# Block 2 of a two-block network: masks behind the level products, inverses turned from the bank, both output gates of seven pairs by quarters

## The chip, the cores and the metric

The kernel runs on one core of a Trainium2 chip. The time is device time in microseconds (us). A core has TensorE (PE in the profile; PEld are its weight loads), VectorE (DVE), ScalarE (ACT), GpSimd (POOL) and SyncE (SP), which issues the loads. They run side by side and wait for one another by semaphores. TensorE writes into eight PSUM banks of 512 f32 per partition, which VectorE and ScalarE read. Everything is f32.

## The reference

The program computes two blocks for 256 tokens of width 1024. The change touches only block 2:

```python
p = jnp.einsum('bsd,de->bse', h, w_in[l])
c_val, c_gate, c_og, ts, r_og, g_conv, g_rwkv = jnp.split(p, SPLITS, axis=-1)
y_conv = _conv_branch(c_val, c_gate, c_og, ...)         # 31 taps, layer norm
y_rwkv = _rwkv7_branch(ts, r_og, ...)                   # the scan below
m = jax.nn.sigmoid(g_conv) * y_conv + jax.nn.sigmoid(g_rwkv) * y_rwkv
x = x + gate[:, None, :] * jnp.einsum('bsd,de->bse', m, w_out[l])

def step(state, inp):                                   # for each token, 16 heads of 64
    r_t, w_t, k_t, v_t, kk_t, b_t = inp
    sk = jnp.einsum('bhvk,bhk->bhv', state, kk_t)
    state = (state * w_t[:, :, None, :] - sk[..., None] * b_t[:, :, None, :]
             + v_t[..., None] * k_t[:, :, None, :])
    return state, jnp.einsum('bhvk,bhk->bhv', state, r_t)
```

## The kernel before, in words

Block 2 goes through eight pairs j = 0 to 7 of heads (128 channels on 128 partitions, 256 tokens along the free side). For each pair nine slices of the input weights, 1024x128 each, are loaded by SyncE into nine slots and multiplied with `hT`, the normed input: VAL and GATE (convolution), R, K, V, OGP and ROG (inner gates), GCP and GRP (the two output gates). `projection` does one of them as 8 matmuls with 256 moving columns and puts the result into bank 0 or 1 by turns (`PLACE`). `read_out` makes it wait until the projection two places earlier has been read out of the bank.

The scan is done in four chunks of 64 tokens. Within a chunk the strictly triangular matrix N of each head is inverted as I + N by doubling, levels 1 to 5. ScalarE copies N from bank 2 to `Nt`. GpSimd makes seven tensors of it (`pool_rwkv`): the first level `Z0` in two operations, and `Nm`, the blocks of N that belong to each level, in five. VectorE transposes `Z0` to `X0` (`turned(0)`). For a level l, TensorE multiplies its blocks with X (`grown(l)`, L1116), VectorE adds the unit matrix (L2449), TensorE multiplies with Z (`inverted(l)`, L1128, at the last level L1130), ScalarE copies what is new of the result from bank 3 to `Xs` (L1633), and VectorE transposes `Xs` to the next Z (`turned(l)`, L2455).

At the same time the pair before, p = j - 1, goes through its four chunks in order (`forced`, `solved`, `outcome` on TensorE; `state` on VectorE, L2442 for the first chunk, multiplies the product S by the decay; `St` is what `forced(c)`, L1064, needs).

`pe_rwkv` is TensorE's queue for a pair, written out by hand: the small products of both pairs in a fixed order, and between them `fill(n)`, which takes n matmuls from the generator `behind`. In pair j this gives the five projections of the next pair (VAL, GATE, K, R, V) and then OGP, ROG, GCP, GRP of its own. The numbers are `FILL = (0, 12, 11, 12, 11, 13, 13)`. Pair 7 has no next pair and fills less. `dve_rwkv` and `act_rwkv` are the queues of VectorE and ScalarE, also written by hand: between the small steps VectorE does the 31 taps of the convolution (`taps`, L2389, 128x256 each with two SBUF inputs), makes the operands of the next pair, and multiplies the inner gates (`og_silu`, `rg_silu`, L2467). ScalarE's queue ends a pair with `half_gate` for GCP and GRP, a tanh out of the bank to `GC` and `GR`. SyncE's queue loads a slot when its projection of the pair before has been done (`load_projection`).

Seven products by quarters are already used in block 1, the feed-forward part and the convolution's output (`quarter_product`, L819; `quarter_sums`, L2121, for the sums of quarters of `hT`).

## Time and profile before

| | us |
|---|---|
| median of 3 runs (1078.93 to 1079.96) | 1079.80 |
| the profiled execution | 1079.88 |
| its span, first to last instruction | 1078.10 |
| TensorE busy | 1065.6 (99%) |
| VectorE busy | 720.0 (67%) |
| ScalarE busy | 235.3 (22%) |
| GpSimd busy | 149.7 (14%) |
| granted TensorE clock, mean | 0.999 |

Block 2 from its first projection to the end of the scan takes about 400 us of the span. A line such as L972 is the line of the kernel before; lines of helpers stand for every caller. In a timeline, start and duration are us from the span's start, x16 is a number of merged instructions, and brackets show how long the engine had been idle and who released it. A recorded matmul's end is modelled, so distances are better read from start to start. Each f32 matmul is two instructions in the trace.

### The profile page before, as it was taken

Reading aid. Unit: us, or ns where it says so; the run is one execution under the profiler, and the core shown is the slowest. Engines: PE = TensorE matmul, PEld = TensorE weight load, DVE = VectorE, ACT = ScalarE, POOL = GpSimd, SP = SyncE. Lnnn points to the kernel's source line nnn. Section 1 sums busy time; section 2 is a strip of 40 time slices with the busy share of each in tenths; the row PEclk is TensorE's granted clock in tenths of the full one; section 3 lists DMA queues with packets and bytes.
Section 4 is the critical chain, followed back from the end, with each engine's and each line's share of the span. In section 5 each row is a group of like instructions: output and inputs, shape, how many; then the busy total and the mean of one; then the engine's idle time right before and its main releaser. Section 6 shows DMA issues by size and latency. Waiting matters only on the chain.

```text
span 1078.1 us, 21003 instructions
## 1 busy us (share of the span) xinstructions
PE 1065.6 (99%) x8606; PEld 910.8 (84%) x8606; DVE 720.0 (67%) x1624; ACT 235.3 (22%) x614; POOL 149.7 (14%) x204
## 2 busy tenths in 40 slices
PE   9999999999999999999999999999999999999997
PEld 7899899998998589999744988888888888887983
DVE  4476674766744377777657768666667667666885
ACT  4131130312210020010101422323232232323101
POOL 1101000000036221100160022020202202020042
PEclk9999999999999999999999999999999999999999
DMA  8676566553347346555446233233332322161251
GB/s 286 236 274 250 188 213 215 161 196 98 138 144 262 124 135 215 193 189 182 168 170 259 79 117 99 89 108 99 99 104 94 111 87 80 27 249 40 79 157 40
DMA packets 62769, 163.20 MB, mean 151 GB/s; under 512 B 8625, under 2 KB 22865, under 8 KB 62674
## 3 DMA queue, kind: packets, MB, share of 16 engines
q1 hardware_dynamic: 61666, 160.22, 44.7%
q8 instruction: 69, 1.13, 0.4%
q10 hardware_dynamic: 1008, 1.63, 0.4%
q14 instruction: 26, 0.21, 0.1%
HBM read 160.73 MB, written 1.11 MB: 150 GB/s over the span
## 4 chain that ended last, share of the span: by engine, by line
PE 91%; DVE 6%; DMA 2%; issue 1%; ACT 0%; DVEq 0%; ACTq 0%
PE bank L819 22%; PE bank L972 20%; PE bank L471 16%; PE bank L885 6%; DVE arena L2389 3%; PE bank L631 3%; PE bank L751 2%; PE bank L794 2%; PE bank L1128 2%; PE bank L1285 2%; PE bank L1116 2%; PE bank L1007 1%; PE bank L947 1%; DMA slots<-in_w_br 1%; PE bank L547 1%; PE bank L953 1%
## 5 line engine op out<-in xcount | busy, mean ns | idle before, releaser
L972 PE MATMUL bank<-hT,slots 128*128 128x256 f32 x1120 | 254.6, 382 | 0.0
L972 PEld LDWEIGHTS bank<-hT,slots 128*128 128x128 f32 x1120 | 209.8, 190 | 28.8
L471 PE MATMUL bank<-hT,slots 128*128 128x256 f32 x544 | 119.7, 379 | 0.0
L471 PEld LDWEIGHTS bank<-hT,slots 128*128 128x128 f32 x544 | 103.0, 190 | 14.4 <-issue 0.6
L2389 DVE SCALAR_TENSOR_TENSOR arena<-padA,par,arena 128x256 f32<-128x256 f32 x232 | 113.9, 552 | 0.0
L819 PE MATMUL bank<-arena,slots 128*128 128x128 f32 x768 | 95.6, 275 | 0.0
L819 PE MATMUL bank<-hT,slots 128*128 128x128 f32 x736 | 91.8, 276 | 0.2 <-DVE arena L1937 0.2
L819 PEld LDWEIGHTS bank<-arena,slots 128*128 128x128 f32 x768 | 90.9, 192 | 0.5
L819 PEld LDWEIGHTS bank<-hT,slots 128*128 128x128 f32 x736 | 86.7, 192 | 1.1 <-issue 1.1
L471 PE MATMUL bank<-arena,slots 128*128 128x256 f32 x304 | 66.5, 380 | 0.5 <-DMA slots<-in_w_br 0.5
L471 PEld LDWEIGHTS bank<-arena,slots 128*128 128x128 f32 x304 | 57.5, 190 | 9.0 <-DMA slots<-in_w_br 1.3
L885 PE MATMUL bank<-slots,arena 128*128 128x512 f32 x128 | 55.4, 592 | 0.0
L2894 POOL TENSOR_TENSOR arena<-arena 128x256 f32<-128x256 f32 x8 | 5.8, 729 | 343.4 <-ACT arena L1650 343.4
L885 PEld LDWEIGHTS bank<-slots,arena 128*128 128x128 f32 x128 | 24.2, 190 | 30.1 <-issue 25.6
L2455 DVE STREAM_TRANSPOSE arena<-arena 128x256 f32<-128x256 f32 x40 | 17.7, 442 | 35.8 <-ACT arena L1633 35.0
L1858 DVE TENSOR_SCALAR arena<-bank 64x256 f32<-64x256 f32 x24 | 10.1, 422 | 38.3 <-PE bank L471 37.9
L2892 POOL TENSOR_TENSOR arena<-arena 128x256 f32<-128x256 f32 x40 | 34.3, 888 | 0.0
L819 PE MATMUL bank<-x,slots 128*128 128x128 f32 x256 | 33.9, 275 | 0.1
L819 PE MATMUL bank<-x,arena 128*128 128x128 f32 x256 | 33.8, 275 | 0.0
L819 PEld LDWEIGHTS bank<-x,slots 128*128 128x128 f32 x256 | 31.2, 192 | 0.3 <-DVE arena L1948 0.3
L819 PEld LDWEIGHTS bank<-x,arena 128*128 128x128 f32 x256 | 31.2, 192 | 0.0
L1902 DVE SCALAR_TENSOR_TENSOR adaA<-arena,sc,adaA 128x1024 f32<-128x1024 f32 x24 | 30.7, 1279 | 0.1
(449 smaller groups left out, 1741.3 us busy)
## 6 DMA issues: line engine op xcount, KB each, us to landing
slots<-in_w_rwkv SPq DMA_DIRECT2D x72, 512.0 KB, 3.6
slots<-in_w_heads SPq DMA_DIRECT2D x68, 512.0 KB, 4.5
slots<-in_w_gu SPq DMA_DIRECT2D x44, 512.0 KB, 4.5
arena<-in_ada_w SPq DMA_DIRECT2D x24, 512.0 KB, 5.4
slots<-in_w_down SPq DMA_DIRECT2D x20, 512.0 KB, 4.3
slots<-in_w_br SPq DMA_DIRECT2D x32, 256.0 KB, 2.8
slots<-in_w_out SPq DMA_DIRECT2D x16, 512.0 KB, 4.1
slots<-in_w_y SPq DMA_DIRECT2D x16, 512.0 KB, 5.2
```

Of the source, the lines that this page charges most:

```text
L471: end = e.matmul(psum, w[:, k * P:(k + 1) * P], rhs[:, k, :], start=k == 0, stop=k == kt - 1)
L631: end = e.matmul(view3(bank[5][:, t * T:(t + 1) * T], P), hT[:, k, t * P:(t + 1) * P], slots[:, BV:CV + 1, k * P:(k + 1) * P], start=k == ...
L751: return e.matmul(bank[DOWN_BANK[m]][:, :], *sides, start=j == 0, stop=j == OUT_PAIRS - 1)
L794: end = e.matmul(psum[:, tokens(t)], w[:, k * P:(k + 1) * P], hT[:, k, tokens(t)], start=k == 0, stop=k == KT - 1)
L819: end = e.matmul(out, w[:, k * P:(k + 1) * P], rhs[:, k, :], start=k == 0, stop=k == 3)
L885: return e.matmul(bank[DOWN_BANK[m]][:, :], *sides, start=j == 0, stop=j == DOWN - 1)
L972: end = e.matmul(proj(w, q), slot[w][:, k * P:(k + 1) * P], hT[:, k, :], start=k == 0, stop=k == KT - 1)
L1116: end = e.matmul(bank[2][r, c * CHUNK:(c + 1) * CHUNK], Nm[r, (l - 1) * CHUNKS + c, :], Xs[r, c, :], start=True, stop=True)
L1128: end = e.matmul(chunks(half(3))[r, c, :], Z[r, c, :], Gs[r, c, :], start=True, stop=True)
L1902: e.scalar_tensor_tensor(out=third, in0=adaW[n % 2], scalar=sc[:, 2 * i + n // 3:2 * i + n // 3 + 1], in1=third, op0=ALU.mult, op1=ALU.add ...
L2389: e.scalar_tensor_tensor(out=o, in0=src, scalar=w, in1=o, op0=ALU.mult, op1=ALU.add).then_inc(*dve.step(f"tap{n}.{q}"))
L2892: e.tensor_tensor(Nm[:, (l - 1) * CHUNKS:l * CHUNKS, :], Nt, each(cst2_of("off", CHUNK, l * CHUNK)), ALU.mult).then_inc(*pool.step(f"Nm{l} ...
```

## The change

Four things, all in block 2.

1. *Gates by quarters, pairs 0 to 6.* GCP and GRP of a pair are no longer two projections but one `own_gate_pair`: the two weight slices and `hT` are each taken as 2x2 quarters, and seven products of 4 matmuls with 128 columns (Winograd's form) take the place of eight. Three go to the first bank, four to the second. VectorE makes four sums of weight quarters per pair (`slice_sum`, 128x512; 0 behind `turned(1)`, 1 and 2 behind `turned(2)`, 3 behind `turned(4)`) and, once, four sums of quarters of `hT` (`bt`) at the end of `dve_first`. ScalarE copies the first product (`bp1`), VectorE adds (`first_quarter` at the end of the pair, `other_quarters` behind `forced(0)` of the next), and ScalarE does both tanh in the next pair, from SBUF, behind its two copies of bank 2. `read_out` waits for these sums. The generator yields every two matmuls: 14 steps for 16.
2. *Masks behind the products.* GpSimd masks N to its strict triangle, adds the unit and makes Z0 of it: three operations. `grown(l)` multiplies with all of I + N, and VectorE's operation behind it multiplies by a mask (`within`) where it added the unit.
3. *Inverses turned from the bank.* `turned(l)` transposes bank 3 and waits for TensorE; ScalarE's copy to `Xs` waits for the transpose.
4. *Loads.* The slot of GCP is reloaded after the end of both gates; the first loads of the output part wait for the last own gates.

```diff
-    put("off_first", (i == t + 1) & (i % 2 == 1))
-    for l in range(LEVELS):
+    put("first", (i == t) | (i == t - 1) & (t % 2 == 1))
+    for l in range(1, LEVELS):
         n = 1 << l
-        c[:, CCOL["off"] + l * CHUNK:CCOL["off"] + (l + 1) * CHUNK] = \
-            (i // (2 * n) == t // (2 * n)) & (i // n % 2 == 0) & (t // n % 2 == 1)
+        at = CCOL["within"] + (l - 1) * CHUNK
+        c[:, at:at + CHUNK] = (i == t) | (i // (2 * n) == t // (2 * n)) & (t // n % 2 == 0) & (i // n % 2 == 1)
...
-        Nm = carve((LEVELS - 1) * CHUNKS, CHUNK)
...
+        bt = [slot[9 + n // 2][:, n % 2 * 512:(n % 2 + 1) * 512].rearrange("p (k n) -> p k n", n=P) for n in range(4)]
+        bs = [slot[11][:, 0:512], slot[11][:, 512:], adaA[:, 2 * D:2 * D + 512]]
+        def own_gates(j, n):
+            at, far = 3 * KT * T + j * T + n * P, KT * T + (P if n == 0 else -P)
+            return arena[:, at:at + 2 * far].rearrange("p (a b) -> p a b", a=2)[:, :, 0:P]
...
+                if w in (GCP, GRP) and q < LAST:
+                    e.wait_ge(*dve.upto(f"bq11.{q}" if w == GCP else f"bq1221.{q}"))
+                elif w in (OGP, ROG, LNSUM, LNVAR):
...
+        def gate_banks_of(q):
+            return [view3(bank[PLACE[w, q] % 2][:, :], P) for w in (GCP, GRP)]
+        def own_gate_pair(e, q):
+            one, two = gate_banks_of(q)
+            low, high = hT[:, 0:4, :], hT[:, 4:8, :]
+            first, second = (slot[w] for w in (GCP, GRP))
+            parts = ((one, 0, first[:, 0:512], low[:, :, tokens(0)]), (one, 1, first[:, 512:], high[:, :, tokens(0)]), (one, 2, bs[0], bt[1]),
+                     (two, 0, second[:, 0:512], bt[0]), (two, 1, bs[1], bt[2]), (two, 2, bs[2], high[:, :, tokens(1)]), (two, 3, second[:, 512:], bt[3]))
+            for n, (out, at, w, rhs) in enumerate(parts):
+                if n == 0:
+                    e.wait_ge(*in_slot[GCP].upto(f"rw{GCP}.{q}"))
+                    read_out(e, PLACE[GCP, q] - 2)
+                if n == 2:
+                    e.wait_ge(*dve.upto("bt4"))
+                    e.wait_ge(*dve.upto(f"bs4.{q}"))
+                if n == 3:
+                    read_out(e, PLACE[GRP, q] - 2)
+                for k in range(4):
+                    end = e.matmul(out[:, at, :], w[:, k * P:(k + 1) * P], rhs[:, k, :], start=k == 0, stop=k == 3)
+                    if k == 3 and n in (2, 6):
+                        end.then_inc(*pe.step(f"b126.{q}" if n == 2 else f"p{GRP}.{q}"))
+                    if k % 2:
+                        yield
...
-                for w in OWN:
+                for w in (OGP, ROG):
                     yield from projection(e, w, j)
+                yield from own_gate_pair(e, j)
...
-                    e.wait_ge(*pool.upto(f"Nm1.{j}"))
+                    e.wait_ge(*pool.upto(f"Nd.{j}"))
...
-                        end = e.matmul(bank[2][r, c * CHUNK:(c + 1) * CHUNK], Nm[r, (l - 1) * CHUNKS + c, :], Xs[r, c, :], start=True, stop=True)
+                        end = e.matmul(bank[2][r, c * CHUNK:(c + 1) * CHUNK], Nt[r, c, :], Xs[r, c, :], start=True, stop=True)
...
-                e.wait_ge(*pe.upto(f"XZ{l}.{j}"))
+                e.wait_ge(*dve.upto(f"Z{l}.{j}"))
...
+            if levels and chain:
+                for w, to in (("gc", GC[:, p, :]), ("gr", GR[:, p, :])):
+                    e.wait_ge(*dve.upto(f"bq1221.{p}"))
+                    e.activation(to, to, ACT.Tanh, scale=0.5).then_inc(*act.step(f"{w}.{p}"))
...
+                    e.wait_ge(*pe.upto(f"b126.{j}"))
+                    e.activation(GC[:, j, P:], gate_banks_of(j)[0][:, 0, :], ACT.Copy).then_inc(*act.step(f"bp1.{j}"))
...
+            quarter_sums(e, bt, "bt", (act.upto("norm4.s3.1"), dve.upto("norm4.s7.1"), pe.upto("lora")))
...
-                e.tensor_tensor(Gs, chunks(half(2)), each(cst2_of("unit")), ALU.add).then_inc(*dve.step(f"G{l}.{j}"))
+                e.tensor_tensor(Gs, chunks(half(2)), each(cst2_of("within", CHUNK, (l - 1) * CHUNK)), ALU.mult).then_inc(*dve.step(f"G{l}.{j}"))
...
+                if l:
+                    e.wait_ge(*pe.upto(f"XZ{l}.{j}"))
+                    e.transpose(flat(Zs[j % 2]), half(3)).then_inc(*dve.step(f"Z{l}.{j}"))
+                else:
+                    e.wait_ge(*pool.upto(f"Z0.{j}"))
+                    e.transpose(flat(Xs), flat(Zs[j % 2])).then_inc(*dve.step(f"X0.{j}"))
...
+                if k == 0:
+                    e.wait_ge(*in_slot[GCP].upto(f"rw{GCP}.{j}"))
+                    e.wait_ge(*in_slot[GRP].upto(f"rw{GRP}.{j}"))
+                    e.tensor_tensor(bs[1], a11, a21, ALU.subtract).then_inc(*dve.step(f"bs3.{j}"))
+                elif k == 1:
+                    e.wait_ge(*dve.upto(f"bs3.{j}"))
+                    e.tensor_tensor(a21, a21, a22, ALU.add).then_inc(*dve.step(f"bs1.{j}"))
+                elif k == 2:
+                    e.wait_ge(*dve.upto(f"bs1.{j}"))
+                    e.tensor_tensor(bs[0], a21, a11, ALU.subtract).then_inc(*dve.step(f"bs2.{j}"))
+                else:
+                    e.wait_ge(*dve.upto(f"bs2.{j}"))
+                    e.tensor_tensor(bs[2], a12, bs[0], ALU.subtract).then_inc(*dve.step(f"bs4.{j}"))
...
+            def first_quarter(q):
+                e.wait_ge(*act.upto(f"bp1.{q}"))
+                e.tensor_tensor(own_gates(q, 0), GC[:, q, P:].unsqueeze(1).to_broadcast([P, 2, P]), gate_banks_of(q)[0][:, 1:3, :],
+                                ALU.add).then_inc(*dve.step(f"bq11.{q}"))
...
+            def other_quarters(q):
+                two = gate_banks_of(q)[1]
+                e.wait_ge(*pe.upto(f"p{GRP}.{q}"))
+                e.wait_ge(*dve.upto(f"bq11.{q}"))
+                e.tensor_tensor(own_gates(q, 1), GR[:, q, P:].unsqueeze(1).to_broadcast([P, 2, P]), two[:, 0:2, :],
+                                ALU.add).then_inc(*dve.step(f"bu43.{q}"))
+                e.wait_ge(*dve.upto(f"bu43.{q}"))
+                e.tensor_tensor(GR[:, q, P:], GR[:, q, 0:P], two[:, 0, :], ALU.add).then_inc(*dve.step(f"bq22.{q}"))
+                e.wait_ge(*dve.upto(f"bq22.{q}"))
+                e.tensor_tensor(own_gates(q, 1), own_gates(q, 1), two[:, 2:4, :], ALU.add).then_inc(*dve.step(f"bq1221.{q}"))
...
+                other_quarters(p)
+                slice_sum(0)
+                slice_sum(2)
+                slice_sum(3)
+                first_quarter(j)
...
-            e.tensor_tensor(Zs[j % 2], Nt, each(cst2_of("off")), ALU.mult).then_inc(*pool.step(f"Z0.m.{j}"))
-            e.wait_ge(*pool.upto(f"Z0.m.{j}"))
-            e.tensor_tensor(Zs[j % 2], Zs[j % 2], each(cst2_of("unit")), ALU.add).then_inc(*pool.step(f"Z0.{j}"))
-            blocks(1)
-            for l in range(2, LEVELS):
-                blocks(l)
+            e.tensor_tensor(Nt, Nt, each(cst2_of("st")), ALU.mult).then_inc(*pool.step(f"Nd.m.{j}"))
+            e.wait_ge(*pool.upto(f"Nd.m.{j}"))
+            e.tensor_tensor(Nt, Nt, each(cst2_of("unit")), ALU.add).then_inc(*pool.step(f"Nd.{j}"))
+            e.wait_ge(*pool.upto(f"Nd.{j}"))
+            e.tensor_tensor(Zs[j % 2], Nt, each(cst2_of("first")), ALU.mult).then_inc(*pool.step(f"Z0.{j}"))
...
-                e.wait_ge(*pe.upto(f"p{w}.{j - 1}" if j else free[w]))
+                e.wait_ge(*pe.upto(f"p{GRP if w == GCP else w}.{j - 1}" if j else free[w]))
...
-            e.wait_ge(*pe.upto("lora"))
+            e.wait_ge(*pe.upto(f"p{GRP}.{LAST - 1}"))
```

## Rows read from the trace of the kernel before

**Rows 1.** The page: its first line, and TensorE's part of the busy times.
```profile
span 1078.1 us, 21003 instructions
...
PE 1065.6 (99%) x8606; PEld 910.8 (84%) x8606; DVE 720.0 (67%) x1624; ACT 235.3 (22%) x614; POOL 149.7 (14%) x204
```
**Rows 2.** Chain that ended last, in order of time: start, us, engine, tile, line, count.
```profile
441.25 6.25 PE bank L819 x56
...
777.76 5.18 PE bank L972 x24
...
801.00 5.81 PE bank L972 x26
```
**Rows 3.** Timeline of TensorE in pair 3, at the first chunk of pair 2.
```profile
766.47 0.63 PE L1116 MATMUL bank<-arena 64*64 64x64 f32 x16
...
767.95 0.33 PE L1064 MATMUL bank<-arena 64*64 64x64 f32 x4 [0.38 <-DVE arena L2442]
...
768.37 0.68 PE L1128 MATMUL bank<-arena 64*64 64x64 f32 x16
```
**Rows 4.** Timeline of TensorE at the same place of pair 7.
```profile
955.51 0.63 PE L1116 MATMUL bank<-arena 64*64 64x64 f32 x16
...
956.76 0.68 PE L1128 MATMUL bank<-arena 64*64 64x64 f32 x16
```
**Rows 5.** Timeline of VectorE in pair 3.
```profile
760.26 0.23 DVE L2435 COPY arena<-bank 128x64 f32<-128x64 f32 x1 [0.82 <-PE bank L1074]
760.88 0.42 DVE L2480 TENSOR_TENSOR arena<-arena,bank 128x256 f32<-128x256 f32 x1 [0.39 <-PE bank L1160]
761.22 2.21 DVE L2389 SCALAR_TENSOR_TENSOR arena<-padA,par,arena 128x256 f32<-128x256 f32 x3
763.36 0.43 DVE L2455 STREAM_TRANSPOSE arena<-arena 128x256 f32<-128x256 f32 x1
763.72 3.98 DVE L2389 SCALAR_TENSOR_TENSOR arena<-padA,par,arena 128x256 f32<-128x256 f32 x6
767.62 0.27 DVE L2442 TENSOR_SCALAR arena<-bank,arena 128x64 f32<-128x64 f32 x1
...
779.42 0.45 DVE L2455 STREAM_TRANSPOSE arena<-arena 128x256 f32<-128x256 f32 x1 [2.78 <-ACT arena L1633]
...
780.67 2.46 DVE L2389 SCALAR_TENSOR_TENSOR arena<-padA,par,arena 128x256 f32<-128x256 f32 x6
...
794.89 0.45 DVE L2455 STREAM_TRANSPOSE arena<-arena 128x256 f32<-128x256 f32 x1 [1.92 <-ACT arena L1633]
...
801.26 0.41 DVE L2467 SCALAR_TENSOR_TENSOR arena<-arena,bank 128x256 f32<-128x256 f32 x1
...
807.12 0.23 DVE L2431 COPY arena<-bank 128x64 f32<-128x64 f32 x1 [1.76 <-PE bank L1066]
```
**Rows 6.** Timeline of GpSimd: all seven operations of pair 3.
```profile
760.61 0.73 POOL L2894 TENSOR_TENSOR arena<-arena 128x256 f32<-128x256 f32 x1 [41.90 <-ACT arena L1650]
761.41 0.87 POOL L2896 TENSOR_TENSOR arena<-arena 128x256 f32<-128x256 f32 x1
762.25 4.38 POOL L2892 TENSOR_TENSOR arena<-arena 128x256 f32<-128x256 f32 x5
```
**Rows 7.** Weight sum and product sum in block 1: ns min/median/max, first and last start.
```profile
L1931 DVE TENSOR_TENSOR arena<-slots,arena x16: 691/692/694, 64.9 to 288.8; 128x512 f32<-128x512 f32 x16
...
L1944 DVE TENSOR_TENSOR arena<-arena,bank x16: 411/420/422, 83.3 to 302.5; 128x256 f32<-128x256 f32 x16
```
**Rows 8.** Timeline of VectorE in pair 0.
```profile
626.63 0.42 DVE L2480 TENSOR_TENSOR arena<-arena,bank 128x256 f32<-128x256 f32 x1 [3.88 <-PE bank L1160]
...
644.77 0.42 DVE L2449 TENSOR_TENSOR arena<-bank,arena 128x256 f32<-128x256 f32 x1 [0.89 <-PE bank L1116]
```
**Rows 9.** Load of slot GRP for pair 3 in SyncE's queue; median landing, page's part 6.
```profile
758.93 0.33 SPq L2944 DMA_DIRECT2D slots<-in_w_rwkv  x1
...
slots<-in_w_rwkv SPq DMA_DIRECT2D x72, 512.0 KB, 3.6
```

More of the change, by code:

```diff
@@ L66 @@
                       ("onehot", 3 * P), ("gmask", 3 * P),
-                      ("off_first", CHUNK), ("off", LEVELS * CHUNK), ("centre", CHUNK), ("unit", CHUNK),
+                      ("first", CHUNK), ("within", (LEVELS - 1) * CHUNK), ("centre", CHUNK), ("unit", CHUNK),
                       ("up", CHUNK), ("st", CHUNK), ("upper_chunks", P), ("cmask", P))
 NKEPT = CCOL["onehot"]
-NFIRST = CCOL["off_first"]
+NFIRST = CCOL["first"]
 def shape_constants():
@@ L959, in read_out @@
                 w, q = ORDER[n]
-                if w in (OGP, ROG, LNSUM, LNVAR):
+                if w in (GCP, GRP) and q < LAST:
+                    e.wait_ge(*dve.upto(f"bq11.{q}" if w == GCP else f"bq1221.{q}"))
+                elif w in (OGP, ROG, LNSUM, LNVAR):
                     e.wait_ge(*dve.upto({OGP: f"og.{q}", ROG: f"rg.{q}", LNSUM: "ln.mean", LNVAR: "ln.ms"}[w]))
@@ L1110, in grown @@
                 else:
-                    e.wait_ge(*pool.upto(f"Nm{l}.{j}"))
                     e.wait_ge(*act.upto(f"X{l - 1}.{j}"))
@@ L1647, in act_rwkv @@
                 e.wait_ge(*pe.upto(f"N.{j}"))
-                if j:
-                    e.wait_ge(*pool.upto(f"Nm{LEVELS - 1}.{j - 1}"))
                 e.activation(Nt, chunks(bank[2][:, 0:T]), ACT.Copy).then_inc(*act.step(f"N.{j}"))
@@ L1709, in act_rwkv @@
             if levels:
-                half_gate(GCP, GC[:, j, :], "gc", j)
                 if more:
-                    half_gate(GRP, GR[:, j, :], "gr", j)
+                    e.wait_ge(*pe.upto(f"b126.{j}"))
+                    e.activation(GC[:, j, P:], gate_banks_of(j)[0][:, 0, :], ACT.Copy).then_inc(*act.step(f"bp1.{j}"))
+                else:
+                    half_gate(GCP, GC[:, j, :], "gc", j)
+                if more:
+                    pass
             else:
@@ L2448, in grown @@
                 e.wait_ge(*pe.upto(f"G{l}.{j}"))
-                e.tensor_tensor(Gs, chunks(half(2)), each(cst2_of("unit")), ALU.add).then_inc(*dve.step(f"G{l}.{j}"))
+                e.tensor_tensor(Gs, chunks(half(2)), each(cst2_of("within", CHUNK, (l - 1) * CHUNK)), ALU.mult).then_inc(*dve.step(f"G{l}.{j}"))
             def turned(l):
-                e.wait_ge(*(act.upto(f"X{l}.{j}") if l else pool.upto(f"Z0.{j}")))
-                to, of, name = (Zs[j % 2], Xs, "Z") if l else (Xs, Zs[j % 2], "X")
-                e.transpose(flat(to), flat(of)).then_inc(*dve.step(f"{name}{l}.{j}"))
+                if l:
[4 more added lines that the diff above has]
+                    e.transpose(flat(Xs), flat(Zs[j % 2])).then_inc(*dve.step(f"X0.{j}"))
             def inverted(l):
@@ L2467, in rg_silu, with slice_sum @@
                 e.scalar_tensor_tensor(out=rg[j % 3], in0=rg[j % 3], scalar=1.0, in1=proj(ROG, j), op0=ALU.add, op1=ALU.mult).then_inc(*dve.step(f"rg.{j}"))
+            def slice_sum(k):
+                a11, a12, a21, a22 = (slot[s][:, columns_half(h)] for s in (GCP, GRP) for h in range(2))
+                if k == 0:
[8 more added lines that the diff above has]
+                    e.tensor_tensor(bs[0], a21, a11, ALU.subtract).then_inc(*dve.step(f"bs2.{j}"))
+                else:
+                    e.wait_ge(*dve.upto(f"bs2.{j}"))
[14 more added lines that the diff above has]
+                e.tensor_tensor(own_gates(q, 1), own_gates(q, 1), two[:, 2:4, :], ALU.add).then_inc(*dve.step(f"bq1221.{q}"))
             if chain:
                 forced(0)
+            if levels and chain:
+                other_quarters(p)
             if end:
@@ L2520, in dve_rwkv @@
             if more:
+                slice_sum(1)
+                slice_sum(2)
                 shift(e, "k", j + 1)
@@ L2604, in dve_rwkv @@
                 taps(e, j + 1, 13 if chain else 10, 18)
+            if more:
+                first_quarter(j)
             if end:
```

4 lines of the change are left out of this document (removed).

## The prediction, made blind

> **What bounds the kernel now.** I read the page first. TensorE is busy for 1065.6 of the 1078.1 us of the span [rows 1]; it is the bound, and only two things can shorten the run: less time on TensorE, or fewer of the 12.5 us in which it stands. So the next views were the chain of work that ended last and TensorE's timeline over one full pair of block 2, here pair 3. The chain gives prices per instruction without a modelled end. Every f32 matmul of the program stands in the trace as two instructions. 24 of them with 256 moving columns take 5.18 us, so 0.2158 us each; 56 with 128 columns take 6.25 us, so 0.1116 us each [rows 2]. One product of seven quarters already exists in the feed-forward part and is exactly those 56.
>
> The timeline of a full pair shows one place where TensorE stands: `forced(1)` (L1064) begins 0.38 us late, released by the VectorE instruction of L2442, `state(1)` [rows 3]. What the stop costs is read by distance: from the start of `grown(1)` (L1116) to the start of `inverted(1)` (L1128) are 768.37 - 766.47 = 1.90 us. In the last pair the same instructions stand between the same two, only without the wait, and take 956.76 - 955.51 = 1.25 us [rows 4]. The stop costs 0.65 us, and it recurs in pairs 1 to 6.
>
> Why is `state(1)` late? The VectorE timeline shows no idle time between the bonus at 760.88 and L2442 at 767.62. Behind the bonus stand nine taps of the convolution (L2389) and one transpose: 2.13 us for the first three taps (761.22 to where the transpose starts), 3.90 us for the next six [rows 5]. The same six taps, later in the same pair, take 2.46 us (at 780.67) [rows 5]. What is different is GpSimd: seven operations run from 760.61 to 762.25 + 4.38 = 766.63 [rows 6]. So beside GpSimd a tap costs 0.65 to 0.71 us, alone 0.41.
>
> **The change, part by part.**
>
> (a) Gates by quarters, pairs 0 to 6. Removed on TensorE: 2 gates x 8 x 2 = 32 instructions of 256 columns, 32 x 0.2158 = 6.91 us. Added: 7 products x 4 x 2 = 56 of 128 columns, 56 x 0.1116 = 6.25 us. Saved: 0.66 us a pair, all on the path, 7 x 0.656 = **4.59 us**. Bounds: a stretch of 26 wide ones between products of 64 rows takes 5.81 us [rows 2], 0.20 more than 26 x 0.2158 = 5.61, so 0.1 at each edge; if each of the 7 groups lost that at its start, nothing would be saved (7 x 0.1 = 0.7). But the row of 56 holds seven groups with their starts, so I take 0.66.
>
> The price is on VectorE. Four weight sums of 128x512 at 0.69 each are 2.77 us a pair; the four that combine the products are three of 0.42 and one of half the width, at most 1.68 [rows 7]. That is 4.4 us more on an engine that is busy for 67% of the span [rows 1] and on which TensorE waits, so it must fall into its gaps:
> - `other_quarters` stands behind `forced(0)`. It takes at most 1.26 us. The gaps there are 0.82 before L2435 and 0.39 before the bonus [rows 5], together 1.21, and each following operation starts some 0.08 before the recorded end of the one before. `solved(0)` moves from 760.26 to 760.5, the bonus stays at 760.9. Nobody waits for that: U0 is next used at 766. If it slips, by 0.1 to 0.2 us.
> - `slice_sum(0)` goes behind `turned(1)`, where the next operation waits for ScalarE anyway; 1 and 2 (1.4 us) stand in the 2.78 us before the transpose at 779.42, which no longer waits for ScalarE's copy of L1633; 3 in the 1.92 us before the one at 794.89 [rows 5].
> - `first_quarter` comes at the pair's end, ahead of 1.76 us of idle time before 807.12 [rows 5] of which the shorter product takes 0.66; 1.1 us are left for its 0.42.
> - `bt` (4 x 0.69 = 2.8 us, once) stands in the 3.88 us before the first bonus [rows 8].
> In pair 0 the gap before level 2 is smaller: 0.89 us before L2449 at 644.77 [rows 8]. The two sums cost 1.4, which is 0.5 more, and the transpose before them comes earlier by ScalarE's copy; between 0 and 0.5, I count +0.2.
>
> (b) Waits that are added on TensorE. The second gate bank is wanted six steps into the product instead of eight: rg must be read out by 801.0 + 3 x 0.45 = 802.3; VectorE reads it out at 801.26 + 0.41 = 801.7 [rows 2, 5]. Slack 0.6, cost nothing; if `rg_silu` came 0.6 us later, TensorE would pay each tenth beyond. The tanh of both gates moves to ScalarE's queue in the next pair, behind the two copies of bank 2; behind it waits `act_value`, whose projection of 16 instructions (16 x 0.2158 = 3.45 us) only begins then. Nothing on the path.
>
> (c) The masks. GpSimd's seven operations become three (mask, unit, first level): from 760.61, with 0.73, 0.87 and 0.87, they end at about 763.2 instead of 766.6. `turned(0)` now waits for the third instead of the second; it starts at 763.36 anyway [rows 5, 6], slack 0.1. The next six taps then run without GpSimd, at 2.46 instead of 3.90. VectorE is ready for `state(1)` at 763.72 + 2.46 = 766.2, about when the product S0 is, which stands in TensorE's queue just ahead of `grown(1)` at 766.47 [rows 3]. St1 is there at 766.7, and TensorE is ready for it at 767.95 - 0.38 = 767.57. G1 is masked between 767.15 and 767.57 (its product ends 766.47 + 0.63), which is the order of the last pair. VectorE has 0.7 us to spare, from the end of `state(1)` at about 766.45 to 767.15. So the stop goes whole: 0.65 x 6 pairs = **3.90 us**. What is late next is G1 itself, by the 0.1 us that is in the 1.25. Bounds: 0 if (a) takes more than that slack and the 0.65, 0.75 if that 0.1 goes too.
> In the last pair the fill ahead of `grown(1)` has 6 steps instead of 12, so `grown(1)` comes 6 x 0.43 = 2.6 us sooner; by the times of pair 3 at 763.9. The third GpSimd operation ends at 763.2 and the transpose behind it at 763.7 [rows 5, 6]: just in time. Two taps stand ahead of the transpose there instead of three, so it begins later than now, and the taps and G1 behind it with it. I count +0.1, bounds 0 and 0.4.
> Mask instead of add behind the products is the same operation with the same operand shapes: nothing.
>
> (d) The inverse is transposed from the bank, and ScalarE's copy X waits for that. Copy and transpose were in series before and are now, in the other order. A transpose out of a bank is not in the trace; the nearest rows are 0.45 for the one from SBUF and the 0.42 of additions that read a bank [rows 5, 7]. I take 0.45, bounds 0.42 to 0.7. Between each Z and the next `grown` lie 5 us of projections, so nothing of it reaches TensorE.
>
> (e) The load of slot GCP waits for the end of both gates. It is issued together with that of GRP at 758.9 [rows 9], no longer ahead of it. Its first user is `slice_sum(0)` at about 769.5 (`inverted(1)` ends at 768.37 + 0.68 [rows 3], the transpose 0.45 later). On SyncE's queue nothing is delayed by it: the load of GRP, behind it, has had this same wait.
>
> Sum, against the profiled execution of 1079.88 us (span 1078.10 and 1.78 around it; the median of the runs is 1079.80): -4.59 - 3.90 + 0.2 + 0.1 = -8.2. **1071.6 us** against the median. A difference of 0.2%, about 2.2 us, is what a measurement of this kernel can tell from none.
>
> **A rule weighed.** Narrow products run here at 0.1116 us for 128 columns against 0.2158 for 256, 52% for half the columns [rows 2]. The Trainium skill, "TensorE: Matmul & The Clock Gate", section "Back-to-back issue gap", says that in a stream of weight loads and matmuls both set the spacing, and gives 81 ns at 128 columns and 131 ns at 512, 62% for a quarter of the columns. By that a cut into quarters loses: an estimate from that page, with 62% in place of 52%, makes (a) a loss of 0.6 us a pair and the whole some 1080. The rows are against it; it is rival 6.
>
> **The rivals.**
> 1. *Only the gates pay.* VectorE is late in front of `state(1)` again: `other_quarters` ahead of U0, the third GpSimd operation ahead of the transpose. From 0.7 us of delay on each further tenth comes back to TensorE; at 1.35 the whole stop is back. For it: both stand in that stretch, and the third GpSimd operation has 0.1 us of slack. Against: the six taps behind the transpose give back 1.4 us. 1079.8 - 4.3 = 1075.5.
> 2. *Narrow products lose at their starts*, interleaved as they are with 64-row products, by up to 0.1 us in each group [rows 2]. Then (a) brings nothing: 1079.8 - 3.6 = 1076.2. Against it: the row of 56.
> 3. *VectorE's queue is stopped by a load* (slower). `slice_sum(0)` stands in the queue ahead of everything that TensorE wants in the rest of the pair, first the copy of U1, a fill of 11 steps (4.8 us) behind `inverted(1)`, so at about 774. It waits for two loads issued at 758.9 [rows 9]. It decides from a landing 15 us after the issue; each microsecond beyond costs 7. With 17.5 us it would be 1071.6 + 7 x 2.5 = 1089. Against it: the median landing of these loads is 3.6 us.
> 4. *It doesn't do what it says:* the quarters leave TensorE's instruction count or widths otherwise than counted, or the masks leave GpSimd as busy. 1079.8.
> 5. *More than counted*: the 0.1 at G1 and small waits elsewhere go too, some 0.3 us a pair: 1069.5.
> 6. *Narrow products are paced by their weight loads.* A load takes 910.8 / 8606 = 0.106 us [rows 1]; it hides under the matmul before. If a quarter of it came on top of each narrow one, 56 x 0.138 = 7.73 us would take the place of 6.91: 1079.8 - 3.6 + 7 x 0.82 = 1081.9. Against it: the row of 56, whose loads are as large.
>
> **How the numbers follow.** Forecast 0.73, rival 1 0.10, rival 2 0.05, rival 3 0.03, rival 4 0.03, rival 5 0.05, rival 6 0.01. The range goes from 1070.0 (0.2 us a pair more than counted) to 1075.8, which takes in rival 1. Faster is the forecast with rivals 1, 2 and 5: 0.93; same is rival 4: 0.03; slower are rivals 3 and 6: 0.04. Of the forecast's own spread (the bounds of (a), (c) and pair 0) some 1070.5 to 1072.6 is likeliest.
>
> **What would show it.** In the profile after: 56 narrow instructions a pair in place of 32 wide ones, the distance from `grown(1)` to `inverted(1)` 1.25 instead of 1.90 us, a pair 1.3 us shorter; no wait at L1064; six taps behind `turned(0)` in 2.5 us; three GpSimd operations, the last over by the time of the transpose; VectorE some 3 us busier a pair. Wrong it would be if the wait at L1064 stays (rival 1), if the 56 take over 6.9 us (rival 2), or if VectorE idles behind `turned(1)` for a DMA (rival 3).

## The result, and the profile after

The kernel after takes **1071.49 us** (median, 1071.29 to 1072.62) beside 1079.37 us of the kernel before in the same series (1078.37 to 1079.96): a ratio of 0.9929, with a 95% interval of 0.9916 to 0.9942. The forecast was 1071.6 us. The profiled execution has a span of 1069.5 us, 8.6 less than before. The top of the page answers to [rows 1]:

```profile
span 1069.5 us, 21375 instructions
PE 1059.4 (99%) x8774; PEld 914.2 (85%) x8774; DVE 740.0 (69%) x1684; ACT 235.8 (22%) x621; POOL 122.9 (11%) x172
```

TensorE has 168 instructions more, which is 7 x (56 - 32), and 6.2 us less to do. VectorE has 20.0 us more than its 720.0 of before; GpSimd has 26.8 us less than its 149.7, with 8 x 4 operations gone. TensorE's granted clock is 9 in every slice of both pages (9 is 90% or more), so the clock plays no part.

The waits of TensorE in block 2 (engine and line, what released it: us in total, times, longest), first before, then after:

```profile
PE bank L1064 <- DVE arena L2442: 2.3, 6, 0.4
```
```profile
PE bank L1009 <- DVE arena L2515: 0.7, 1, 0.7
```

The stop that the prediction set out to remove (`forced(1)`) is gone in all six pairs. A new one stands in its place, once.

TensorE's timeline of pair 3 at the same spot (start, duration, engine, line, tiles, count) answers to [rows 3]. The lines moved: `grown` is L1154, `forced` L1103, `inverted` L1166.

```profile
763.14 0.63 PE L1154 MATMUL bank<-arena 64*64 64x64 f32 x16
...
764.08 0.28 PE L1103 MATMUL bank<-arena 64*64 64x64 f32 x4
...
764.39 0.68 PE L1166 MATMUL bank<-arena 64*64 64x64 f32 x16
```

`forced(1)` carries no wait, and from `grown(1)` to `inverted(1)` are 764.39 - 763.14 = 1.25 us, where 1.90 were.

VectorE's timeline of the same pair answers to [rows 5], and shows why:

```profile
757.89 2.22 DVE L2433 SCALAR_TENSOR_TENSOR arena<-padA,par,arena 128x256 f32<-128x256 f32 x3
760.03 0.43 DVE L2503 STREAM_TRANSPOSE arena<-arena 128x256 f32<-128x256 f32 x1
760.39 2.42 DVE L2433 SCALAR_TENSOR_TENSOR arena<-padA,par,arena 128x256 f32<-128x256 f32 x6
763.12 0.28 DVE L2487 TENSOR_SCALAR arena<-bank,arena 128x64 f32<-128x64 f32 x1 [0.32 <-PE bank L1128]
...
773.19 0.45 DVE L2500 STREAM_TRANSPOSE arena<-bank 128x256 f32<-128x256 f32 x1 [0.53 <-PE bank L1166]
```

The six taps behind the first transpose take 2.42 us instead of 3.98, and `state(1)` (L2487) now waits 0.32 us for TensorE, not TensorE for it. The last row is the transpose of level 2, now out of a bank: 0.45 us, as from SBUF. GpSimd's timeline answers to [rows 6], and is over before the six taps begin:

```profile
757.28 0.73 POOL L2978 TENSOR_TENSOR arena<-arena 128x256 f32<-128x256 f32 x1 [44.06 <-ACT arena L1686]
758.09 0.86 POOL L2980 TENSOR_TENSOR arena<-arena 128x256 f32<-128x256 f32 x1
759.03 0.79 POOL L2982 TENSOR_TENSOR arena<-arena 128x256 f32<-128x256 f32 x1
```

**Where the time went.** The bonus product begins each pair, so its starts mark the pairs off (timelines of TensorE; L1160 before, L1198 after). Before, they are 625.90, 664.76, 712.23, 760.14 and so on to 951.78; after, 624.89, 664.04, 710.22, 756.82 and so on to 943.24:

| stretch | before | after | difference |
|---|---|---|---|
| up to the first bonus (block 2 begins 1.01 earlier) | 625.90 | 624.89 | -1.01 |
| pair 0 | 38.86 | 39.15 | +0.29 |
| pair 1 | 47.47 | 46.18 | -1.29 |
| pairs 2 to 6, each | 47.91 | 46.60 | -1.31 |
| last pair and output | 126.32 | 126.26 | -0.06 |

-1.01 + 0.29 - 1.29 - 5 x 1.305 - 0.06 = -8.6. The first 1.01 us is not of the change: block 2 itself begins at 606.56 before and at 605.55 after, in code that is the same in both, and in the profiled executions of the eight kernels below, whose code up to there is the same again (but for the sums `bt`, which masks_and_turns lacks), the first bonus lies anywhere between 623.74 and 625.48. So about -7.6 us is the change's by this account, -7.9 by the medians.

### The profile page after: what moved, and what is told of

It reads as the page before. It is cut to its first block, busy times and chain, and to the rows that moved or that the text cites. A ratio compares the mean times of both kernels' runs of the same rounds, so it can differ in the third digit from the quotient of the medians.

```text
span 1069.5 us, 21375 instructions
## 1 busy us (share of the span) xinstructions
PE 1059.4 (99%) x8774; PEld 914.2 (85%) x8774; DVE 740.0 (69%) x1684; ACT 235.8 (22%) x621; POOL 122.9 (11%) x172
## 3 DMA queue, kind: packets, MB, share of 16 engines
q10 hardware_dynamic: 1008, 1.63, 0.4%
## 4 chain that ended last, share of the span: by engine, by line
PE 97%; DVE 1%; DMA 1%; issue 0%; ACT 0%; POOL 0%; DVEq 0%; ACTq 0%; POOLq 0%
PE bank L828 23%; PE bank L983 18%; PE bank L480 17%; PE bank L894 6%; PE bank L1009 4%; PE bank L640 3%; PE bank L760 2%; PE bank L803 2%; PE bank L1154 2%; PE bank L1166 2%; PE bank L1323 2%; PE bank L956 1%; PE bank L1045 1%; PE bank L556 1%; PE bank L962 1%; PE bank L1023 1%
## 5 line engine op out<-in xcount | busy, mean ns | idle before, releaser
L983 PE MATMUL bank<-hT,slots 128*128 128x256 f32 x896 | 204.5, 382 | 0.0
L983 PEld LDWEIGHTS bank<-hT,slots 128*128 128x128 f32 x896 | 167.8, 190 | 23.2 <-issue 0.3
L480 PE MATMUL bank<-hT,slots 128*128 128x256 f32 x544 | 119.7, 379 | 0.0
L480 PEld LDWEIGHTS bank<-hT,slots 128*128 128x128 f32 x544 | 103.0, 190 | 14.4 <-issue 0.6
L2433 DVE SCALAR_TENSOR_TENSOR arena<-padA,par,arena 128x256 f32<-128x256 f32 x232 | 102.9, 504 | 0.0
L828 PEld LDWEIGHTS bank<-hT,slots 128*128 128x128 f32 x736 | 86.7, 192 | 1.0 <-issue 0.9
L2978 POOL TENSOR_TENSOR arena<-arena 128x256 f32<-128x256 f32 x8 | 5.9, 732 | 359.8 <-ACT arena L1686 359.8
L640 PE MATMUL bank<-slots,hT 128*128 128x256 f32 x128 | 28.9, 379 | 0.0
L1555 ACT ACTIVATE arena<-bank 128x128 f32<-128x128 f32 x20 | 5.6, 278 | 104.7 <-PE bank L828 99.5
```

Of the source, the lines that this page charges most:

```text
L480: end = e.matmul(psum, w[:, k * P:(k + 1) * P], rhs[:, k, :], start=k == 0, stop=k == kt - 1)
L640: end = e.matmul(view3(bank[5][:, t * T:(t + 1) * T], P), hT[:, k, t * P:(t + 1) * P], slots[:, BV:CV + 1, k * P:(k + 1) * P], start=k == ...
L828: end = e.matmul(out, w[:, k * P:(k + 1) * P], rhs[:, k, :], start=k == 0, stop=k == 3)
L983: end = e.matmul(proj(w, q), slot[w][:, k * P:(k + 1) * P], hT[:, k, :], start=k == 0, stop=k == KT - 1)
L2433: e.scalar_tensor_tensor(out=o, in0=src, scalar=w, in1=o, op0=ALU.mult, op1=ALU.add).then_inc(*dve.step(f"tap{n}.{q}"))
```

## The experiments

The pairs are the ruler in what follows: "a pair" is the distance between the bonus products of pairs 3 and 4. A full pair takes 47.91 us before and 46.60 us after, and within one profile full pairs repeat to 0.02 us, while whole runs of one kernel differ by 1 to 2.5 us. Ratios are against the kernel before on the same chip. The line numbers move by a few from kernel to kernel; the text gives the names.

| kernel | us, median | ratio, 95% interval | a pair |
|---|---|---|---|
| masks_and_turns | 1075.15 | 0.9959 (0.9945 to 0.9973) | 47.26 |
| gates_alone | 1082.29 | 1.0025 (1.0016 to 1.0034) | 48.29 |
| copy_first | 1077.95 | 0.9990 (0.9980 to 0.9999) | 47.64 |
| gpsimd_busy | 1075.76 | 0.9965 (0.9952 to 0.9978) | 47.25 |
| rg_early | 1070.35 | 0.9917 (0.9904 to 0.9931) | 46.60 |
| two_more_sums | 1071.53 | 0.9927 (0.9914 to 0.9941) | 46.61 |
| four_more_sums | 1071.10 | 0.9926 (0.9912 to 0.9940) | 46.60 |
| eight_more_sums | 1074.36 | 0.9958 (0.9944 to 0.9972) | 46.97 |

**One part at a time.** masks_and_turns is the kernel before with the new masks and the transposes out of the bank, and its wide gates. gates_alone is the kernel before with the gates by quarters, and neither of the other parts: GpSimd has its seven operations again. The edits are shortened here.

```diff
 # masks_and_turns: against the kernel after
-                for w in (OGP, ROG):
+                for w in OWN:
                     yield from projection(e, w, j)
-                yield from own_gate_pair(e, j)
...
 # gates_alone: against the kernel after
-                e.tensor_tensor(Gs, chunks(half(2)), each(cst2_of("within", CHUNK, (l - 1) * CHUNK)), ALU.mult)
+                e.tensor_tensor(Gs, chunks(half(2)), each(cst2_of("unit")), ALU.add)
-                    e.wait_ge(*pe.upto(f"XZ{l}.{j}"))
-                    e.transpose(flat(Zs[j % 2]), half(3))
+                    e.wait_ge(*act.upto(f"X{l}.{j}"))
+                    e.transpose(flat(Zs[j % 2]), flat(Xs))
...
+            for l in range(2, LEVELS):
+                blocks(l)
...
```

> Parts 2 and 3 of the change alone: three GpSimd operations, masks behind the products, inverses turned from the bank; both output gates stay whole projections. Theory (GpSimd's seven operations slow nine taps, and that makes state(1) late): the stop at forced(1) goes in pairs 1 to 6, 6 x 0.65 = 3.9 us, so about 1075.5 against 1079.4; the distance from grown(1) to inverted(1) falls from 1.90 to 1.25 us and a full pair from 47.91 to 47.26 us. Rival (the stop has another cause and only the gates pay): 1079.4, distance 1.90.

> Part 1 of the change alone: quarters for both output gates of seven pairs, with the seven GpSimd operations, the unit added and the transposes behind ScalarE's copy as before. Theory (VectorE has room for the sums only where the other parts make it): the gates save 0.66 a pair on TensorE, but the stop of 0.65 stays, and the transpose at level 2 still waits for ScalarE's copy, so that two weight sums push VectorE's chain about 1.5 us past the point where TensorE wants F2 and G3; the run is no faster than before, about 1079 to 1084. Rival (the parts are independent): 1079.4 - 4.6 + 0.8 for the wait at rg in pair 0 = 1075.6.

masks_and_turns takes 47.26 us a pair, 0.65 less than before, and TensorE has no wait left in block 2. That is the stop at `forced(1)` to the hundredth. From there to the kernel after are 47.26 - 46.60 = 0.66 us: the quarters, to the hundredth too.

But the quarters alone make the kernel **slower**, by 0.25%, and a pair by 0.38 us, although TensorE has the same 0.66 us a pair less to do. The waits of TensorE in block 2 of gates_alone:

```profile
PE bank L1114 <- DVE arena L2480: 4.4, 6, 0.7
PE bank L1104 <- DVE arena L2491: 2.2, 6, 0.4
PE bank L1010 <- DVE arena L2516: 0.7, 1, 0.7
PE bank L1168 <- DVE arena L2498: 0.4, 1, 0.4
```

The second row is the old stop. The first is new: behind `grown(3)` the product of L1114 (`solved(2)` of the pair before) waits six times for `F2` (L2480), VectorE's copy of what `forced(2)` gave, which comes late. The fourth is in pair 0, at `inverted(3)`. The work added to VectorE for the quarters doesn't fit, as long as the other two parts aren't there. The next two kernels ask which of them makes the room.

**Without the transpose from the bank.** copy_first is the kernel after, except that ScalarE copies X out of the bank first and VectorE transposes that copy, as before the change.

```diff
-                    e.wait_ge(*pe.upto(f"XZ{l}.{j}"))
-                    e.transpose(flat(Zs[j % 2]), half(3))
+                    e.wait_ge(*act.upto(f"X{l}.{j}"))
+                    e.transpose(flat(Zs[j % 2]), flat(Xs))
             def inverted(l):      # on ScalarE
-                e.wait_ge(*dve.upto(f"Z{l}.{j}"))
+                e.wait_ge(*pe.upto(f"XZ{l}.{j}"))
```

> The changed kernel, but ScalarE copies X first and VectorE transposes the copy, as before; masks, three GpSimd operations and quarters stay. Theory (turning from the bank is what makes room for weight sums 1 and 2, and for 3): at level 2 the transpose starts at ScalarE's copy, 2.2 us later than now, 0.6 us of idle time before F2 takes up a part, so 1.3 to 1.6 us of TensorE waiting a pair in six pairs, and some 0.4 more at level 5: 1079 to 1083, and TensorE waits for VectorE behind L1105 and L1154 at level 3. Rival (the order of copy and transpose does not matter, since both were in series before): 1071.5.

A pair takes 47.64, 1.04 us more than after, and the stop at `F2` is there as in gates_alone. The mechanism is the one expected; the time, 1077.95 us, is below the range, and the 0.4 us that was expected at level 5 didn't come (a wait of 0.4 us stands once, in pair 0). No wait is listed at `forced(1)`: the new masks take the old stop away without the new transpose too. VectorE, ScalarE and TensorE in pair 3, in that order:

```profile
776.66 0.45 DVE L2500 STREAM_TRANSPOSE arena<-arena 128x256 f32<-128x256 f32 x1 [2.78 <-ACT arena L1671]
777.03 0.65 DVE L2523 TENSOR_TENSOR slots<-slots 128x512 f32<-128x512 f32 x1
777.72 0.69 DVE L2526 TENSOR_TENSOR slots<-slots 128x512 f32<-128x512 f32 x1
...
779.25 2.46 DVE L2433 SCALAR_TENSOR_TENSOR arena<-padA,par,arena 128x256 f32<-128x256 f32 x6
781.63 0.41 DVE L2390 TENSOR_TENSOR arena<-arena 128x256 f32<-128x256 f32 x1
781.96 0.21 DVE L2476 COPY arena<-bank 128x64 f32<-128x64 f32 x1
```
```profile
775.48 0.38 ACT L1630 ACTIVATE arena<-bank 128x256 f32<-128x256 f32 x1 [5.47 <-PE bank L983]
...
776.36 0.28 ACT L1671 ACTIVATE arena<-bank 128x128 f32<-128x128 f32 x1
```
```profile
782.23 0.33 PE L1113 MATMUL bank<-arena 64*64 64x64 f32 x4 [0.72 <-DVE arena L2476]
```

ScalarE's copy (L1671) takes 0.28 us, but it comes at 776.36, because it stands in ScalarE's queue behind an operation that waited 5.47 us for a projection of TensorE. The transpose on VectorE waits 2.78 us for it, and two sums and six taps are queued behind the transpose, ahead of `F2`. In the kernel after the transpose starts at 773.19; copy_first runs 1.22 us later as a whole at that point (its bonus product stands at 758.04, not 756.82), so the transpose is 776.66 - 1.22 - 773.19 = 2.25 us earlier in the kernel after, and `F2` has time to spare:

```profile
775.97 2.46 DVE L2433 SCALAR_TENSOR_TENSOR arena<-padA,par,arena 128x256 f32<-128x256 f32 x6
778.35 0.42 DVE L2390 TENSOR_TENSOR arena<-arena 128x256 f32<-128x256 f32 x1
779.39 0.23 DVE L2476 COPY arena<-bank 128x64 f32<-128x64 f32 x1 [0.63 <-PE bank L1105]
```

These are rows of the kernel after, VectorE: `F2` (L2476) waits for TensorE. The order can't simply be dropped, with both engines reading the bank at once: the Trainium skill, "PSUM — Partial Sum Buffer", section "PSUM bank collisions raise a hardware error", says that two different engines on one bank and the same partitions at the same time raise an error and can read wrong data. No run here tried it; in the kernel after ScalarE's copy waits for the transpose.

**With GpSimd busy.** gpsimd_busy is the kernel after with four more multiplications behind GpSimd's three, into memory that nobody reads (only ScalarE's next copy of N, a pair later, waits for them; not shown).

```diff
             e.tensor_tensor(Zs[j % 2], Nt, each(cst2_of("first")), ALU.mult)
+            for n in range(4):
+                e.tensor_tensor(spare[:, n * CHUNKS:(n + 1) * CHUNKS, :], Nt, each(cst2_of("st")), ALU.mult)
```

> The changed kernel with four more GpSimd operations of 128x256 behind Z0, whose results nobody reads, so that GpSimd is as busy as before and nothing waits for it longer. Theory (contention between GpSimd and the taps): the six taps behind turned(0) take 3.9 instead of 2.4 us, state(1) is late again, and TensorE waits at forced(1) and inverted(1): 0.5 to 0.8 us a pair in pairs 1 to 6, so about 1075.4 (1074.3 to 1076.3). Rival (the waits for the masks counted, not the busy engine): 1071.5, taps 2.4 us.

A pair takes 47.25, 0.65 us more, and TensorE waits for `state(1)` again. GpSimd, VectorE and TensorE in pair 3:

```profile
760.46 3.51 POOL L2987 TENSOR_TENSOR arena<-arena 128x256 f32<-128x256 f32 x4
```
```profile
761.07 3.98 DVE L2436 SCALAR_TENSOR_TENSOR arena<-padA,par,arena 128x256 f32<-128x256 f32 x6
764.96 0.27 DVE L2490 TENSOR_SCALAR arena<-bank,arena 128x64 f32<-128x64 f32 x1
```
```profile
765.29 0.33 PE L1104 MATMUL bank<-arena 64*64 64x64 f32 x4 [0.38 <-DVE arena L2490]
```

Four GpSimd operations whose result has no reader bring back the 3.98 us of the six taps and the 0.38 us of the wait, both exactly as in [rows 3, 5]. So what the masks save they save through VectorE's pace: without it nothing of the 0.65 us is left. In the last pair, where the kernel before had no such wait [rows 4], one of 0.25 us comes up too. The two losses also add up: 1.04 (copy_first) + 0.65 (gpsimd_busy) = 1.69 = 48.29 - 46.60, the distance of gates_alone from the kernel after.

**The new wait in pair 0.** In the kernel after `rg_silu` of pair 0, which reads out the bank that the second gate needs, stands behind taps and `grown(5)`. rg_early moves it ahead of the taps.

```diff
                 if not chain:
+                    rg_silu()
                     taps(e, j + 1, 6, 10)
...
             if more:
-                rg_silu()
+                if chain:
+                    rg_silu()
                 operand_r(e, j + 1)
```

> The changed kernel, but in pair 0 VectorE does rg_silu before four of its taps instead of behind the last inverse. Theory (TensorE stands for 0.79 us at the second gate bank of pair 0 because rg is read out too late there): the wait at L1009 goes, 0.7 us off, about 1070.8. Rival (the next thing in VectorE's queue, G5, is late by as much): 1071.5 and a wait of 0.3 us or more at inverted(5).

Pair 0 takes 38.38 us instead of 39.15, and no wait is left in block 2. Only the pairs can tell the two kernels apart: 1070.35 and 1071.49 us are 0.8% and 0.7% below before, with intervals that overlap. Its pair 0 on TensorE, and behind it that of the kernel after with VectorE's two operations ahead of the wait:

```profile
658.19 0.66 PE L1168 MATMUL bank<-arena 64*64 64x32 f32 x16
658.77 2.05 PE L1009 MATMUL bank<-slots 128*128 128x128 f32 x16
```
```profile
657.59 0.65 PE L1168 MATMUL bank<-arena 64*64 64x32 f32 x16
658.96 2.05 PE L1009 MATMUL bank<-slots 128*128 128x128 f32 x16 [0.72 <-DVE arena L2515]
```
```profile
658.29 0.29 DVE L2507 COPY arena<-bank 128x128 f32<-128x128 f32 x1 [0.76 <-PE bank L1168]
658.50 0.41 DVE L2515 SCALAR_TENSOR_TENSOR arena<-arena,bank 128x256 f32<-128x256 f32 x1
```

From the last level's product (L1168) to the gate's: 0.58 us with rg early, 1.37 without.

**How much room VectorE has.** The three kernels add two, four and eight additions of 128x256 out of the second gate bank, ahead of the last quarter's, and are otherwise the kernel after.

```diff
                 e.tensor_tensor(GR[:, q, P:], GR[:, q, 0:P], two[:, 0, :], ALU.add)
+                for n in range(4):               # 2, 4 or 8
+                    e.tensor_tensor(spare[n], GC[:, 0:2, 0:P], two[:, 0:2, :], ALU.add)
```

> The changed kernel with two more additions of 128x256 (bank and SBUF) per pair inside other_quarters, read by nobody: about 0.7 to 0.8 us more on VectorE ahead of solved(0). Theory (idle time of 0.20 + 0.32 + 0.42 us stands in VectorE's chain between the bonus and G1, 0.94 us of slack): no change, 1071.5, within 0.5. Rival (slack of 0.2 to 0.3 us only, one thin gap): 0.5 us a pair, 1074.5.

> The same with four more additions, about 1.4 to 1.5 us. Theory (slack of 0.94): 0.5 us too much a pair, less what the taps win by running later, when GpSimd is done: 0.2 to 0.5 us in each of six pairs, so 1072.7 to 1074.5, seen at L1103 or L1166. Rival (thin gap): 1.2 us a pair, 1078.5.

> The kernel after with eight VectorE additions of 128x256 out of the second gate bank where four were put before, results unused, just ahead of the last quarter's addition. Four cost nothing (1071.10 us; pair 46.60): 1.32 us of work went in, of which 0.48 came back because three taps moved out from beside GpSimd (their row 2.22 became 1.74) and 0.32 was idle time ahead of the state scaling at L2488, which then followed the taps with no idle time, ending at 763.01 where TensorE began the products that read it at 763.65. Theory (VectorE's room ahead of that point is what was left there, about 0.5 us, and then each further us stops TensorE): four more add 1.32; the three taps give back at most another 0.45, so the scaling comes 0.9 to 1.3 later and TensorE stops for 0.3 to 0.9 us a pair in seven pairs: 1073.5 to 1077.5 us, pair 46.9 to 47.5, and the wait is listed at L1104 against the DVE state row. Rival (VectorE as a whole isn't near any limit, since it is idle a quarter of the pair, and later work closes up): 1071 to 1072 us, pair 46.60.

Two cost nothing, as expected. Four, 1.3 us, cost nothing either, which was not expected: the room was taken to be the 0.94 us of idle time in three gaps, and too little was counted for the taps. Eight cost 0.37 us a pair, as expected, though TensorE's wait isn't in the list at L1104: it shows as distance only. VectorE in pair 3, with four and with eight:

```profile
756.26 1.41 DVE L2550 TENSOR_TENSOR arena<-arena,bank 128x256 f32<-128x256 f32 x4
...
758.38 1.74 DVE L2434 SCALAR_TENSOR_TENSOR arena<-padA,par,arena 128x256 f32<-128x256 f32 x3
760.03 0.43 DVE L2504 STREAM_TRANSPOSE arena<-arena 128x256 f32<-128x256 f32 x1
```
```profile
757.63 2.73 DVE L2550 TENSOR_TENSOR arena<-arena,bank 128x256 f32<-128x256 f32 x8
...
761.07 1.27 DVE L2434 SCALAR_TENSOR_TENSOR arena<-padA,par,arena 128x256 f32<-128x256 f32 x3
762.25 0.45 DVE L2504 STREAM_TRANSPOSE arena<-arena 128x256 f32<-128x256 f32 x1
```

The three taps ahead of the transpose take 2.22 us in the kernel after, 1.74 with four sums and 1.27 with eight. The sums push them out from beside GpSimd's three operations, which don't move (in pair 3 the second starts 1.26 to 1.27 us behind the bonus product in all three kernels). The room can now be added up. Eight sums put `L2552` (the addition behind them) 2.85 us behind the one ahead of them, instead of 0.32 in the kernel after: 2.53 us more. Of these the gap before the bonus takes 0.29, the taps give back 0.96 (1.18 us from their start to the transpose's, instead of 2.14), and the idle time ahead of `state(1)` takes 0.39. `state(1)` is 0.88 us later against `grown(1)`, and TensorE pays 0.38 of that: from `grown(1)` to `inverted(1)` are 1.63 us instead of 1.25:

```profile
764.09 0.63 PE L1155 MATMUL bank<-arena 64*64 64x64 f32 x16
...
765.72 0.68 PE L1167 MATMUL bank<-arena 64*64 64x64 f32 x16
```

So VectorE has 2.53 - 0.38 = 2.15 us of room there, where the prediction had written 0.7 for (c) alone. With four sums, which put 1.21 us more between the same two, the first three terms take all but 0.04. That is the room of a full pair. The last pair, whose fill is shorter, has less: from its bonus product to the projection behind `inverted(2)` eight sums make it 11.62 us (945.67 to 957.29) instead of 10.19 (943.24 to 953.43), so 1.4 us on TensorE at once.

## Why the prediction was right, and where it was not

**(a) The quarters: right in size, incomplete as a condition.** 0.656 us a pair was forecast and 0.66 measured (masks_and_turns against the kernel after). The chain of the kernel after answers to [rows 2] with 12 instructions in 1.34 us and 44 in 5.11:

```profile
793.75 1.34 PE bank L1009 x12
797.07 5.11 PE bank L1009 x44
```

That is 6.45 us, 0.2 more than the 6.25 of the row in block 1; but those two stretches have edges against other products, and so had the 26 wide ones of [rows 2] (5.81 instead of 5.61). Rival 2 (starts of groups lose) and rival 6 (paced by weight loads) are out: either would have left less than 0.66. The Trainium skill's figures in "TensorE: Matmul & The Clock Gate", section "Back-to-back issue gap", 81 ns at 128 columns and 131 ns at 512, don't carry over to these f32 products: here 128 columns take 1.34 / 12 = 0.1117 us and 256 take 0.2158.

**VectorE's extra work.** The forecast was "some 3 us" a pair; by the busy time from bonus to bonus (pair 2) it is 36.44 instead of 33.89, so 2.6. That it falls into gaps is right only with (d), see there.

**(b) The rg wait: wrong for pair 0.** The step reads "Slack 0.6, cost nothing". It was worked out at 801 us, in a full pair, and holds there. Pair 0 has another order of work: its own fill numbers (`FILL_FIRST`, 14, 9, 9, 10, 10 and 10) have used 62 steps by its last level, exactly where the second gate bank begins, while VectorE has `rg_silu` behind that level's copy. The wait is 0.72 us in the list and 0.79 by distance, and rg_early takes back 0.77. The prediction's own warning ("if `rg_silu` came 0.6 us later, TensorE would pay") names the mechanism, but was never held against the one pair that differs.

**(c) The masks: right.** 0.65 us in six pairs, and the stop goes whole. gpsimd_busy shows the cause by bringing it back. The two terms for the pairs that differ didn't come. In pair 0, at the gap of 0.89 us [rows 8], TensorE's `grown(3)` and `inverted(3)` stand 644.28 - 643.03 = 1.25 us apart, 1.21 before: 0.04 instead of 0.2, as the transpose ahead of the two sums starts earlier. (In copy_first, where the transpose waits for ScalarE's copy as before, TensorE waits 0.40 us there.) In the last pair VectorE did what was said: the transpose (L2503) waits for GpSimd, then two taps follow. The row (kernel after):

```profile
946.27 0.45 DVE L2503 STREAM_TRANSPOSE arena<-arena 128x256 f32<-128x256 f32 x1 [0.62 <-POOL arena L2982]
```

But TensorE's distance from `grown(1)` to `inverted(1)` stays 948.22 - 946.97 = 1.25 us, so it costs 0, the lower bound, instead of 0.1.

**(d) The transpose from the bank: the operation right, its worth wrong.** The duration taken, 0.45 us, is the one measured. But the step was costed at nothing: copy and transpose "were in series before and are now, in the other order". By duration that is so. By queue it is not: ScalarE's copy was late, behind an operation that waits for a projection, and VectorE's queue stood behind that copy. Turning first gives VectorE 2.25 us of room, and without it the quarters' sums cost 1.04 us a pair: about 6 us in six pairs, more than the 4.59 the quarters bring. The sum came out right since (a) had already put two weight sums into those 2.78 us, "which no longer waits for ScalarE's copy". What was missing was the statement that (a) hangs on (d). Rival 1, "only the gates pay", didn't come, but its price was right as long as (d) is there: gpsimd_busy is that state, and its pair of 47.25 us is 47.91 less the 0.66 of the quarters. Without (d) the quarters don't pay at all, as gates_alone shows.

(d) isn't quite free either. In pair 0, from the product at 646.72 (L1253) to `grown(4)` at 649.96 TensorE takes 3.24 us instead of 3.11; it is 3.24 in masks_and_turns too, and 3.11 and 3.12 in copy_first and gates_alone, so it comes with (d). The likely reason, not tested by itself, is that ScalarE's copy, and what ScalarE does next, comes later behind the transpose.

**(e) The later load:** nothing, as forecast. The transposes are followed at once by the weight sums, with no wait for a DMA, so rival 3 didn't come.

**The sum.** Put together again with what was measured: -0.66 x 7 = -4.6 for the quarters, -0.65 x 6 = -3.9 for the stop, +0.8 for rg in pair 0 makes -7.7, against -8.2 forecast, -7.6 by the pairs and -7.9 by the medians. Pair 0 closes to the hundredth: -0.66 for the quarters, +0.79 for rg, +0.04 at `inverted(3)` and +0.12 from (d) make the +0.29 of the table. The forecast of 1071.6 us lies 0.1 us from 1071.49, with one term missed (+0.8) and two counted that didn't come (+0.3). That closeness is luck: the saving was put 0.3 us too high, and the kernel before, counted as 1079.80, measured 1079.37 beside the kernel after.

## What to carry to other kernels

When an edit that saves time on the bound engine costs time on another, ask which other part of the same change makes the room for it: alone, the quarters made this kernel slower, and with it they gave all they promised in every full pair. A step whose operations only swap places isn't priced by their durations; read what stands ahead of each in its engine's queue. And work every slack out in the iterations that differ, the first and the last, not only in the steady one; the order of work there is another, and what this change lost on TensorE it lost in the first pair; the last pair has the least room for more.
